# A two-layer Hyena, attention and experts kernel: Hyena filters computed in the head and at the joint, one column pass per group of modulation sections, the convolution's layer norm inside attention

## The chip, the cores and the metric

The kernel runs on one core of one Trainium2 chip. The metric is the device time of one execution in microseconds; the time before the change is 1821.3 us, the median of three runs (1820.79 to 1822.10). All arithmetic is in 32-bit floats.

## What is computed

Two layers work on 384 tokens of width 1024: 128 context tokens and 256 latent tokens, that is three tiles of 128 (NT = 3). Cut to what matters here, a layer is:

```python
mod = cond @ w_mod + b_mod                       # 6 sections of 1024, for two conditions
sh1, sc1, g1, sh2, sc2, g2 = split(mod, 6)
h = rms_norm(x) * (1 + sc1) + sh1
y = mixer(h)                                     # three groups side by side, then w_out
x = x + g1 * rms_norm(y)
h = rms_norm(x) * (1 + sc2) + sh2
x = x + g2 * rms_norm(moe(h))                    # 64 experts, 8 per token, and a shared one

# mixer: u = h @ w_in, cut into the columns of three groups
# convolution: a = u1 * sigmoid(u2); depthwise conv, 31 taps; layer_norm; silu
# Hyena: short conv; z = gate * (irfft(rfft(z) * kf) + bias * z), twice
# attention: four heads, difference of two softmaxes, rms_norm
# kf, from weights alone:
hid  = sin(fr * (feats @ hy_w1 + hy_b1))
hid  = sin(fr * (hid @ hy_w2 + hy_b2))
filt = (hid @ hy_w3) * window                    # forward and backward
kf   = rfft([fwd, 0, reversed bwd])
```

The Hyena filter and its spectrum depend on a layer's weights and on nothing else.

## The kernel before

Five engines run written-out programs, joined by semaphores; each program is in order. The work of a layer falls into stages.

**Modulation.** w_mod comes in 24 chunks of 2 MB (12 a layer), two for each section. `mod_chunk` (L616) multiplies a chunk by the padded condition (COND, 32 columns) into banks 6 and 7 of PSUM, four row groups of 32; after a section's second chunk ScalarE copies the rows out (`mod_rows`, L1271), TensorE folds them into columns with eight matmuls against FOLD (`mod_columns`, L606, "a column pass") and ScalarE copies the columns (`mod_column`, L1280). Chunks 0 to 3 (shift and scale of layer 0) are done in the head, chunks 4 to 15 in the attention of layer 0 (`fill`, L341: one chunk per unit) and 16 to 23 in that of layer 1. Their buffers are slot 0 of RING and KSYS in turn; SyncE reloads one once the chunk two before is used (`mod_in`, L381).

**Hyena filter.** `hidden` (L632, L1286, L1698) is one sine layer: a matmul, four VectorE operations and a Sin. `filters` (L641, L1708) makes the filter of one tile: two matmuls, then four VectorE operations with the windows, and the next tile's matmuls wait for them, since both use banks 1 and 2. `spectra` (L652, L1291) is the transform by matmuls, copied to KSYS by ScalarE. In layer 0 `hidden` runs in the head, in layer 1 behind the first two column tiles; in both layers `filters` stands behind tiles 2 to 4 and `spectra` behind tiles 5 to 7.

**Column tiles.** `u_tile` (L813) makes w_in's 19 outputs: ten in feature order with 128x384 results, nine in token order with 128x512. Between them stand the Hyena transforms (`z_turn`, `z_spectra`, `z_conv`), the mean and the variance of the convolution's layer norm (`conv_mean`, L713) and the turning of queries and keys (`qk_turn`). VectorE does the short convolution, the 31 taps, the rotary embedding and the gates.

**Layer norm of the convolution** (L1870 to L1888 on VectorE, L1371 to L1375 on ScalarE). It stands in front of attention in both programs: variance plus EPS, Sqrt on ScalarE, reciprocal, multiply, gain and bias, Sigmoid on ScalarE, multiply.

**Attention.** Twelve units (three tiles, four heads) in a pipeline of 14 iterations (L1093, L1377, L1890). An iteration of TensorE: scores of unit i, transpose of the weights of unit i - 1, column pass if there is one, a modulation chunk, pieces of w_out, values of unit i - 1, transpose of the output of unit i - 2. The scores of unit i wait for the exponentials of unit i - 1. GpSimd takes the power -0.5 of one column per unit (`power`, L509).

**Joint.** After the experts of layer 0, the sums of squares, the three residuals, the three normalisations and the transposes into feature order (`y_mean`, `residual`, `normalise`, `features`) lead to the first column tile of layer 1. GpSimd clears CB and RW there (`pads`, L575), behind its powers.

**Experts.** 34 steps a layer with 64 experts of 3 MB, the weights loaded during the steps. GpSimd makes a 128x384 comparison per step (`scat`, L522).

## Time and profile before

| What | us |
|---|---|
| median of three runs | 1821.3 |
| span of the profiled execution | 1822.1 |
| that execution's own time | 1823.92 |
| TensorE (PE) busy | 1705.8 (94%) |
| VectorE (DVE) busy | 617.4 (34%) |
| ScalarE (ACT) busy | 377.0 (21%) |
| GpSimd (POOL) busy | 187.2 (10%) |

Read it by stage: one share for the whole span is an average over stages in which different things are waited for. In the timelines a row is a start, a duration, an engine, the line and operation, what it writes and reads, how often, and in brackets how long the engine had been idle and what released it. A 32-bit matmul shows as two records.

### The profile page before, as it was taken

To read this page: it belongs to the slowest core of one execution; us is meant where nothing else is said; L and a number is where in the kernel's file an instruction comes from. 1 tells how busy PE (TensorE), PEld (TensorE's weight loads), DVE (VectorE), ACT (ScalarE), POOL (GpSimd) and SP (SyncE) were. 2 spreads that over 40 slices of the span, in tenths; PEclk is the share of its full clock that TensorE was granted. 3 is DMA by queue.
4 is the path that set the end of the run, shared out by engine and by line. 5 is a ranking of instruction groups with operands and counts; after the bars stand their busy time and mean duration, and the time that the engine had idled before them with its cause. 6 is when DMAs were issued, how large, how long until landed. Compare 5 with 4: busy or idle time off the path is not lost.

```text
span 1822.1 us, 22136 instructions
## 1 busy us (share of the span) xinstructions
PE 1705.8 (94%) x8440; PEld 824.3 (45%) x8440; DVE 617.4 (34%) x1669; ACT 377.0 (21%) x850; POOL 187.2 (10%) x193
## 2 busy tenths in 40 slices
PE   4999799989999999999959997999999999999995
PEld 2555345544444444444435553555444444444442
DVE  1358342422222222222154673433222222222223
ACT  2210343211111111111131014431111111111111
POOL 1000000011111111111110000100111111111110
PEclk9999889999999999999979998998999999999998
DMA  9212581198999999999832137315799999999993
GB/s 398 93 74 93 206 337 69 58 374 338 425 409 418 426 405 422 426 426 426 352 127 93 54 131 263 118 47 213 320 415 425 404 425 412 417 425 426 426 425 135
DMA packets 77147, 541.00 MB, mean 297 GB/s; under 512 B 8304, under 2 KB 11376, under 8 KB 21488
## 3 DMA queue, kind: packets, MB, share of 16 engines
q1 hardware_dynamic: 67248, 503.90, 67.4%
q0 software_dynamic: 9792, 35.66, 4.8%
q8 instruction: 69, 1.13, 0.2%
q14 instruction: 38, 0.31, 0.0%
HBM read 533.76 MB, written 5.77 MB: 296 GB/s over the span
## 4 chain that ended last, share of the span: by engine, by line
PE 87%; DMA 6%; DVE 3%; ACT 2%; issue 1%; SPq 0%; ACTq 0%; POOL 0%; DVEq 0%
PE PSB L836 29%; PE PSB L845 14%; PE PSB L828 7%; PE PSB L823 6%; PE PSB L890 5%; PE PSB L891 5%; PE PSB L791 4%; PE PSB L878 4%; PE PSB L626 2%; DMA RING<-in_wmod 2%; PE PSB L863 1%; DMA X<-in_x 1%; DMA WB<-in_exp_w_up 1%; DMA RING<-in_exp_w_up 1%; DMA KSYS<-in_wmod 1%; PE PSB L852 1%
## 5 line engine op out<-in xcount | busy, mean ns | idle before, releaser
L836 PE MATMUL PSB<-WB,EX 128*32 128x512 f32 (+2 forms) x1408 | 432.1, 598 | 0.2 <-DMA RING<-in_exp_w_up 0.2
L836 PE MATMUL PSB<-RING,EX 128*32 128x512 f32 (+2 forms) x1344 | 417.3, 598 | 3.8 <-DMA WB<-in_exp_w_up 2.1
L845 PE MATMUL PSB<-RING,AT 128*32 128x512 f32 (+2 forms) x720 | 229.8, 602 | 4.9 <-issue 3.8
L1647 DVE TENSOR_TENSOR YL<-PSB,YH 128x512 fp32r<-128x512 f32 x136 | 94.1, 692 | 354.5 <-ACT YH L1246 354.5
L845 PE MATMUL PSB<-WB,AT 128*32 128x512 f32 (+2 forms) x704 | 210.8, 596 | 0.0
L890 PE MATMUL PSB<-YH,SCAT 128*128 128x512 f32 x408 | 172.1, 422 | 2.8 <-DVE YL L1647 2.8
L836 PEld LDWEIGHTS PSB<-WB,EX 128*32 128x32 f32 (+2 forms) x1408 | 113.1, 126 | 136.0 <-issue 136.0
L526 POOL TENSOR_SCALAR SCAT<-CST,LSTT 128x384 fp32r<-128x384 f32 x68 | 85.2, 1252 | 841.6 <-PE PSB L891 841.5
L836 PEld LDWEIGHTS PSB<-RING,EX 128*32 128x32 f32 (+2 forms) x1344 | 105.8, 124 | 124.8 <-issue 124.8
L891 PE MATMUL PSB<-YL,SCAT 128*128 128x512 f32 x408 | 161.2, 395 | 0.0
L1629 DVE COPY EX<-PSB 128x512 f32<-128x512 f32 x68 | 47.0, 692 | 323.4 <-PE PSB L878 323.4
L1246 ACT ACTIVATE YH<-PSB 128x512 fp32r<-128x512 f32 x136 | 81.2, 597 | 239.6 <-PE PSB L845 239.6
L828 PE MATMUL PSB<-RING,HT 128*128 128x512 f32 x288 | 125.6, 592 | 0.0
L823 PE MATMUL PSB<-HT,RING 128*128 128x384 f32 x320 | 109.0, 495 | 3.3 <-ACT HT L1191 3.3
L878 PEld LDWEIGHTS PSB<-CST,XG 128*128 128x128 f32 x544 | 58.8, 141 | 106.9 <-issue 106.9
L845 PEld LDWEIGHTS PSB<-RING,AT 128*32 128x32 f32 (+2 forms) x720 | 63.5, 130 | 79.2 <-issue 79.2
L512 POOL TENSOR_TENSOR ST<-ST,HALF 128x1 f32<-128x1 f32 x48 | 26.4, 550 | 654.1 <-DVE ST L1911 476.6
L845 PEld LDWEIGHTS PSB<-WB,AT 128*32 128x32 f32 (+2 forms) x704 | 58.4, 126 | 72.4 <-issue 71.9
L1239 ACT ACTIVATE SGM<-PSB 128x256 f32<-128x256 f32 x68 | 26.1, 384 | 312.5 <-PE PSB L836 312.5
L878 PE MATMUL PSB<-CST,XG 128*128 128x128 f32 x544 | 88.2, 285 | 0.0
L890 PEld LDWEIGHTS PSB<-YH,SCAT 128*128 128x128 f32 x408 | 77.7, 190 | 21.6 <-issue 4.9
L791 PE MATMUL PSB<-RING,YT 128*128 128x512 f32 x192 | 85.0, 593 | 0.0
(262 smaller groups left out, 1779.0 us busy)
## 6 DMA issues: line engine op xcount, KB each, us to landing
RING<-in_exp_w_gate SPq DMA_DIRECT2D x64, 1024.0 KB, 10.5
RING<-in_exp_w_up SPq DMA_DIRECT2D x64, 1024.0 KB, 13.6
RING<-in_exp_w_down SPq DMA_DIRECT2D x64, 1024.0 KB, 14.1
WB<-in_exp_w_gate SPq DMA_DIRECT2D x64, 1024.0 KB, 11.8
WB<-in_exp_w_up SPq DMA_DIRECT2D x64, 1024.0 KB, 14.4
WB<-in_exp_w_down SPq DMA_DIRECT2D x64, 1024.0 KB, 14.1
RING<-in_wmod SPq DMA_DIRECT2D x14, 2048.0 KB, 10.0
KSYS<-in_wmod SPq DMA_DIRECT2D x10, 2048.0 KB, 9.3
```

What stands on the lines that cost most here:

```text
L526: nc.gpsimd.tensor_scalar(SCAT[:, s % 2, :], cst("iota"), LSTT[:, s:s + 1], None, ALU.is_equal).then_inc(p_scat, 1)
L791: mm = nc.tensor.matmul(PS[YB[0][t] + hf][:, :], YT[:, f, t * P:(t + 1) * P], w[:, f, :], start=(f == 0), stop=(f == 7))
L823: mm = nc.tensor.matmul(PS[3 + i % 3][:, 0:TOK], w[:, k, :], HT[:, k, :], start=(k == 0), stop=(k == KD - 1))
L828: mm = nc.tensor.matmul(PS[3 + i % 3][:, :], HT[:, k, t * P:(t + 1) * P], w[:, k, :], start=(k == 0), stop=(k == KD - 1))
L836: mm = nc.tensor.matmul(PS[6][s0:s0 + w, :].rearrange("p (w f) -> p w f", w=2), e[:, k, s0:s0 + w], rawgu[n % NBUF][:, k], start=(k == 0), ...
L845: mm = nc.tensor.matmul(dst[s0:s0 + w, :], AT[:, j, s0:s0 + w], rawdn[n % NBUF][:, hf, j], start=(j == 0), stop=(j == 1))
L878: mm = nc.tensor.transpose(PS[7][:, c * P:(c + 1) * P], XG[:, s % 2, k * P:(k + 1) * P], ident)
L890: nc.tensor.matmul(PS[piece][:, :], w, YHb[s % 2][:, cols], start=False, stop=False, skip_group_check=True)
L891: mm = nc.tensor.matmul(PS[piece][:, :], w, YLb[s % 2][:, cols], start=False, stop=True, skip_group_check=True)
L1246: sc.activation(YHb[s % 2][:, hf * 512:(hf + 1) * 512], PS[6 + hf][:, :], ACT.Copy).then_inc(a_yh, 1)
L1629: v.tensor_copy(EX2[:, s % 2, 4:8, :].rearrange("p k s -> p (k s)"), PS[7][:, :]).then_inc(e_high, 1)
L1647: v.tensor_tensor(YLb[s % 2][:, hf * 512:(hf + 1) * 512], PS[6 + hf][:, :], YHb[s % 2][:, hf * 512:(hf + 1) * 512].bitcast(F32), ALU.subtr ...
```

## The change

It has four parts.

1. The Hyena hidden layers, filters and spectra leave the column-tile stage. In layer 0 they stand between the four modulation chunks of the head, and the parameters are loaded ahead of the first chunk; in layer 1 the hidden layers, filters and the first spectrum stand between the steps of the joint, in banks 6 and 7, and the two other spectra behind the first two column tiles.
2. The modulation sections are taken in four groups (0 to 1, 2 to 5, 6 to 7, 8 to 11). The chunks of a group add into the same banks, each section's condition shifted to other rows, and a group has one copy of the rows and one column pass, with FOLD of up to eight columns.
3. The layer norm's end moves into the attention: GpSimd takes the power -0.5 of the variance (128x384) in one operation in place of Sqrt and reciprocal; VectorE normalises in iteration 4 (and applies gain and bias); ScalarE takes the exponential of the negative in iteration 5; VectorE makes 1/(1 + e) times the value in iterations 6 and 7, one half of the channels in each.
4. GpSimd clears only the padding columns, and for layer 1 right behind the experts, ahead of its powers of the joint.

```diff
-        COND = sb("COND", [P, KD, MT])
-        FOLD = sb("FOLD", [P, 2])
+        COND = sb("COND", [P, KD, MT + 6])
+        FOLD = sb("FOLD", [P, 8])
-        FTB = ((6, 0, 2), (4, 4, 4))
+        FTB = (((2, 6, 0), (4, 4, 4)), ((0, 2, 4), (4, 4, 4)))
+        HB = (0, 6)
+        SECS = ((0, 2), (2, 6), (6, 8), (8, 12))
 # SyncE
+                    sp.dma_start(PR[:, :], I["par"][0]).then_inc(par_in, 16)
                     mod_in(0)
-                    sp.dma_start(PR[:, :], I["par"][0]).then_inc(par_in, 16)
                     mod_in(1)
 # GpSimd
-                own.sig(nc.gpsimd.memset(CB[:, :, :], 0.0), p_pad)
-                own.sig(nc.gpsimd.memset(RW[:, :, :], 0.0), p_pad)
+                for first in (0, CPAD + P, 2 * CPAD + TOK):
+                    own.sig(nc.gpsimd.memset(CB[:, :, first:first + CPAD], 0.0), p_pad)
+                for first in (0, 1 + P, 2 + TOK):
+                    own.sig(nc.gpsimd.memset(RW[:, :, first:first + 1], 0.0), p_pad)
...
             for l in range(DEPTH):
+                pool.wait_ge(d_ln, K_LN * l + 5)
+                own.sig(nc.gpsimd.tensor_tensor(SG[:, 0, :], SG[:, 1, :], HALF[:, 0:1].to_broadcast([P, TOK]), ALU.pow), p_pow)
                 for u in range(NUN):
                     power(d_oms, NUN * l + u + 1, 24 + 2 * (u % 2), 1)
...
                 mixture_pool(l)
+                if l + 1 < DEPTH:
+                    pads()
 # TensorE
-            def mod_columns(sec):
+            def mod_columns(g):
+                first, last = SECS[g]
+                n = 2 * (last - first)
...
                 for k in range(KD):
-                    mm = nc.tensor.matmul(PS[5][:, 2 * k:2 * k + 2], MROWS[sec > 1][:, sec % 2, k * P:(k + 1) * P], FOLD[:, :],
+                    mm = nc.tensor.matmul(PS[5][:, n * k:n * (k + 1)], MROWS[g][:, k * P:(k + 1) * P], FOLD[:, 0:n],
...
+                at = 6 - 2 * (sec - first)
+                elif sec == first and part == 0:
+                    pe.wait_ge(a_mod, 2 * g)
-                        mm = nc.tensor.matmul(PS[6 + hf][MT * c:MT * (c + 1), :], COND[:, 4 * part + c, :],
-                                              w[:, c, hf * 512:(hf + 1) * 512], start=(part == 0), stop=(part == 1))
+                        mm = nc.tensor.matmul(PS[6 + hf][MT * c:MT * (c + 1), :], COND[:, 4 * part + c, at:at + MT],
+                                              w[:, c, hf * 512:(hf + 1) * 512], start=(sec == first and part == 0),
+                                              stop=(sec == last - 1 and part == 1), skip_group_check=True)
...
                 if l == 0:
                     pe.wait_ge(const_in, 16)
+                    hidden(l, 0)
+                    hidden(l, 1)
                     mod_chunk(0)
+                    filters(l, 0)
+                    filters(l, 1)
                     mod_chunk(1)
-                    hidden(l, 0)
-                    mod_columns(0)
+                    filters(l, 2)
+                    spectra(l, 0)
                     mod_chunk(2)
-                    hidden(l, 1)
+                    spectra(l, 1)
+                    spectra(l, 2)
                     mod_chunk(3)
-                    mod_columns(1)
-                    pe.wait_ge(d_arg, 8)
-                for t in range(NT):
-                    to_features(l, 0, t)
+                    mod_columns(0)
+                    to_features(l, 0, 0)
+                    to_features(l, 0, 1)
+                    pe.wait_ge(a_spec, 6 * (l + 1))
+                    to_features(l, 0, 2)
+                else:
+                    hidden(l, 0)
+                    hidden(l, 1)
+                    for t in range(NT):
+                        filters(l, t)
+                        to_features(l, 0, t)
+                    spectra(l, 0)
                 features_done(l, 0, 2)
                 for i in range(19):
                     u_tile(l, i)
                     if l > 0 and i < 2:
-                        hidden(l, i)
-                    if 2 <= i < 5:
-                        filters(l, i - 2)
-                    if 5 <= i < 8:
-                        spectra(l, i - 5)
+                        spectra(l, i + 1)
 # ScalarE, layer 1: hidden() behind the squares of y tiles 1 and 2; before attention gone:
-                act.wait_ge(d_ln, K_LN * l + 5)
-                own.sig(sc.activation(SG[:, 0, :], SG[:, 1, :], ACT.Sqrt), a_ln)
-                act.wait_ge(d_ln, K_LN * l + 10)
-                for c in range(2):
-                    own.sig(sc.activation(SG[:, c, :], CN[:, c, :], ACT.Sigmoid), a_ln)
...
+                    if i == 5:
+                        act.wait_ge(d_ln, K_LN * l + 9)
+                        for c in range(2):
+                            own.sig(sc.activation(SG[:, c, :], CN[:, c, :], ACT.Exp, scale=-1.0), a_ln)
-                    if j is not None and j % 2 == 1:
-                        mod_rows(j // 2)
+                    if j is not None and j + 1 in (12, 16, 24):
+                        mod_rows(GROUP[j // 2])
 # VectorE, layer 1, the joint
+                    scalars()
+                    hidden(l, 0)
+                    y_mean(l - 1, 1, 0)
                     modulation(l, 0, 2, MODR)
                     scale(0)
-                    y_mean(l - 1, 1, 0)
                     y_mean(l - 1, 1, 1)
                     residual(l - 1, 1, 0)
                     y_mean(l - 1, 1, 2)
+                    hidden(l, 1)
                     residual(l - 1, 1, 1)
                     normalise(l, 0, 0)
+                    filters(l, 0)
                     residual(l - 1, 1, 2)
                     normalise(l, 0, 1)
                     features(l, 0, 0)
+                    filters(l, 1)
                     normalise(l, 0, 2)
                     features(l, 0, 1)
+                    filters(l, 2)
                     features(l, 0, 2)
-                    scalars()
 # VectorE, layer norm
-                dve.wait_ge(a_ln, 3 * l + 1)
-                do(v.reciprocal(SG[:, 1, :], SG[:, 0, :]), d_ln)
...
+                def late_norm(n):
+                    if n == 0:
+                        dve.wait_ge(p_pow, POW[l, "cn"][0])
+                        for c in range(2):
+                            sig(v.tensor_tensor(CN[:, c, :], CN[:, c, :], SG[:, 0, :], ALU.mult), d_ln)
+                        own.wait(d_ln)
+                        for c in range(2):
+                            sig(v.tensor_scalar(CN[:, c, :], CN[:, c, :], par("lng")[:, c:c + 1], par("lnb")[:, c:c + 1],
+                                                ALU.mult, ALU.add), d_ln)
+                        return
+                    c = n - 1
+                    dve.wait_ge(a_ln, 2 * (l + 1))
+                    do(v.tensor_scalar(SG[:, c, :], SG[:, c, :], 1.0, None, ALU.add), d_ln)
+                    do(v.reciprocal(SG[:, c, :], SG[:, c, :]), d_ln)
+                    sig(v.tensor_tensor(YT[:, c, :], CN[:, c, :], SG[:, c, :], ALU.mult), d_ln)
...
+                    if i in (4, 6, 7):
+                        late_norm((4, 6, 7).index(i))
```

## Rows read from the trace of the kernel before

**Rows 1.** Busy time of each engine by stage; then granted clock, DMA share, GB/s.
```profile
0.00:50.00 50.00, 24.59 (x124) 12.38 (x124) 12.64 (x37) 14.58 (x30) 4.73 (x10) 0.97 0.95 388
50.00:204.50 154.50, 153.01 (x468) 84.02 (x469) 83.25 (x178) 20.56 (x49) 0.00 (x0) 1.00 0.23 85
204.50:290.00 85.50, 72.01 (x446) 35.75 (x447) 36.42 (x116) 37.22 (x119) 6.58 (x12) 0.84 0.78 295
...
390.00:919.00 529.00, 523.77 (x2904) 231.16 (x2903) 132.76 (x359) 86.46 (x170) 74.24 (x65) 1.00 0.96 401
919.00:945.00 26.00, 6.54 (x29) 5.24 (x28) 18.81 (x38) 13.11 (x31) 6.06 (x8) 0.61 0.56 222
```

**Rows 2.** TensorE's timeline in the head: chunk 1, chunk 3, first column tiles.
```profile
22.27 3.64 PE L626 MATMUL PSB<-RING,COND 128*32 128x512 f32 x16 [3.73 <-DMA RING<-in_wmod]
...
38.23 1.92 PE L626 MATMUL PSB<-RING,COND 128*32 128x512 f32 x16
...
50.09 15.72 PE L823 MATMUL PSB<-HT,RING 128*128 128x384 f32 x48 [1.81 <-ACT HT L1191]
```

**Rows 3.** Chain of waits, layer 0: hidden layer, one filter step, one spectrum.
```profile
37.52 0.80 PE PSB L639 x2
...
65.80 1.92 PE PSB L648 x4
...
94.50 3.43 PE PSB L665 x8
```

**Rows 4.** VectorE's timeline: parameters' first use, a hidden layer, one filter.
```profile
17.43 0.14 DVE L1811 TENSOR_SCALAR ST<-PR 64x1 f32<-64x1 f32 x1 [7.10 <-DMA PR<-in_par]
...
27.49 0.67 DVE L1703 TENSOR_SCALAR CO<-PSB,ST 64x384 f32<-64x384 f32 x1 [8.82 <-PE PSB L636]
...
29.17 0.35 DVE L1706 TENSOR_SCALAR CO<-CO 64x384 f32<-64x384 f32 x1
...
67.83 0.69 DVE L1714 TENSOR_TENSOR QKV<-PSB,CST 128x512 f32<-128x512 f32 x1 [16.67 <-PE PSB L648]
...
69.76 0.68 DVE L1717 TENSOR_TENSOR QKV<-QKV 128x512 f32<-128x512 f32 x1
```

**Rows 5.** SyncE's issues of modulation chunks in layer 0's attention.
```profile
218.85 0.35 SPq L388 DMA_DIRECT2D KSYS<-in_wmod  x1
225.13 0.33 SPq L388 DMA_DIRECT2D RING<-in_wmod  x1
```

**Rows 6.** Timeline of the joint, VectorE, GpSimd, TensorE.
```profile
935.26 0.75 DVE L1449 TENSOR_SCALAR YT<-X,ST 128x1024 f32<-128x1024 f32 x1 [0.73 <-POOL ST L512]
...
938.08 3.17 DVE L1449 TENSOR_SCALAR YT<-X,ST 128x1024 f32<-128x1024 f32 x1 [0.73 <-POOL ST L512]
938.67 2.04 POOL L578 MEMSET RW<- 128x2322 f32 x1
...
944.79 7.22 PE L823 MATMUL PSB<-HT,RING 128*128 128x384 f32 x16 [1.51 <-ACT HT L1191]
```

**Rows 7.** Timeline of layer 0's attention, VectorE and TensorE.
```profile
206.35 2.55 DVE L1879 RECIPROCAL SG<-SG 128x384 f32<-128x384 f32 x1 [12.76 <-ACT SG L1372]
...
214.46 0.80 PE L1100 MATMUL PSB<-KT,QT 64*128 64x128 f32 x4 [7.60 <-ACT HT L1389]
...
219.72 1.85 PE L612 MATMUL PSB<-FOLD,CO 128*128 128x2 f32 x16
...
232.98 3.64 PE L626 MATMUL PSB<-RING,COND 128*32 128x512 f32 x16 [1.34 <-DMA RING<-in_wmod]
...
278.08 1.92 PE L626 MATMUL PSB<-KSYS,COND 128*32 128x512 f32 x16 [1.09 <-DMA KSYS<-in_wmod]
```

**Rows 8.** GpSimd's groups of the whole span: count, busy us, mean ns, idle before.
```profile
L526 POOL TENSOR_SCALAR SCAT<-CST,LSTT 128x384 fp32r<-128x384 f32 x68 | 85.2, 1252 | 841.6 <-PE PSB L891 841.5
...
L512 POOL TENSOR_TENSOR ST<-ST,HALF 128x1 f32<-128x1 f32 x48 | 26.4, 550 | 654.1 <-DVE ST L1911 476.6 <-DVE ST L1462 110.3 <-DVE ST L1447 67.2
```

More of the change, by code:

```diff
@@ L339, in build @@
         SLOT_OF = {key: (a, i + 1) for a, use in enumerate(SLOT_USE) for i, key in enumerate(use)}
+        SECS = ((0, 2), (2, 6), (6, 8), (8, 12))
+        GROUP = {s_: g_ for g_, (a_, b_) in enumerate(SECS) for s_ in range(a_, b_)}
         def fill(l, i):
             first, n = (4, 12) if l == 0 else (16, 8)
-            return first + i if i < n else None, (first + i) // 2 - 1 if 0 < i <= n and i % 2 == 0 else None
+            ended = {8: 1, 12: 2} if l == 0 else {8: 3}
+            return first + i if i < n else None, ended.get(i)
         def pieces(l, i):
@@ L618, in mod_chunk @@
                 a, n = SLOT_OF["m", j]
-                part = j % 2
+                sec, part = divmod(j, 2)
+                g = GROUP[sec]
+                first, last = SECS[g]
+                at = 6 - 2 * (sec - first)
                 if j == 0:
                     pe.wait_ge(d_cond, 3)
+                elif sec == first and part == 0:
+                    pe.wait_ge(a_mod, 2 * g)
                 pe.wait_ge(chunk_in[a], 16 * n)
@@ L647, in filters @@
                 for half in range(2):
-                    mm = nc.tensor.matmul(PS[1 + half][:, :], HID[:, 4, t * P:(t + 1) * P],
+                    mm = nc.tensor.matmul(PS[HB[l] + half][:, :], HID[:, 4, t * P:(t + 1) * P],
                                           par("w3", 64)[:, half * 512:(half + 1) * 512], start=True, stop=True)
@@ L660, in spectra @@
                         w = cst("cf1" if part == 0 else "sf1")
-                        mm = nc.tensor.matmul(PS[1 + part][:, :], w, f[:, 0, :], start=True, stop=True)
+                        mm = nc.tensor.matmul(PS[HB[l] + part][:, :], w, f[:, 0, :], start=True, stop=True)
                     else:
@@ L664, in spectra @@
                         for t in range(2):
-                            mm = nc.tensor.matmul(PS[1 + part][:, :], w[:, t, (q - 1) * P:q * P], f[:, 1 + t, :],
+                            mm = nc.tensor.matmul(PS[HB[l] + part][:, :], w[:, t, (q - 1) * P:q * P], f[:, 1 + t, :],
                                                   start=(t == 0), stop=(t == 1))
@@ L1294, in spectra @@
                 for part in range(2):
-                    own.sig(sc.activation(KS[:, q, part, :, :].rearrange("p o n -> p (o n)"), PS[1 + part][:, :], ACT.Copy), a_spec)
+                    own.sig(sc.activation(KS[:, q, part, :, :].rearrange("p o n -> p (o n)"), PS[HB[l] + part][:, :], ACT.Copy), a_spec)
             def z_out(l, o):
@@ L1332, in _ @@
                 if l == 0:
+                    hidden(l, 0)
+                    hidden(l, 1)
                     for t in range(NT):
                         squares(l, 0, t)
+                    for q in range(NT):
+                        spectra(l, q)
                     mod_rows(0)
-                    hidden(l, 0)
                     mod_column(0)
-                    hidden(l, 1)
-                    mod_rows(1)
-                    mod_column(1)
                     act.wait_ge(d_mod, 3)
@@ L1347, in _ @@
                             y_squares(l - 1, 1, t, hf)
+                        if t > 0:
+                            hidden(l, t - 1)
                     squares(l, 0, 0)
@@ L1354, in _ @@
                     features(l, 0, 2)
+                    spectra(l, 0)
                 act.wait_ge(d_fr, 5 * (l + 1))
                 own.sig(sc.activation(ST[:, 34:36], ST[:, 32:34], ACT.Exp), a_lam)
[L1358 removed]
+                act.wait_ge(p_pad, 6 * (l + 1))
                 for i in range(19):
@@ L1361, in _ @@
                     if l > 0 and i < 2:
-                        hidden(l, i)
-                    if 5 <= i < 8:
-                        spectra(l, i - 5)
+                        spectra(l, i + 1)
                     if i in (8, 13):
@@ L1820, in _ @@
                     hidden(l, 0)
+                    hidden(l, 1)
+                    for t in range(NT):
+                        filters(l, t)
                     for t in range(NT):
                         normalise(l, 0, t)
-                    hidden(l, 1)
                     modulation(l, 0, 2, MODC)
@@ L1834, in _ @@
                     y_mean(l - 1, 1, 2)
+                    hidden(l, 1)
                     residual(l - 1, 1, 1)
                     normalise(l, 0, 0)
+                    filters(l, 0)
                     residual(l - 1, 1, 2)
```

90 lines of the change are left out of this document (39 added, 51 removed).

## The prediction

> **What bounds the kernel now.** I read the busy table by stage first [rows 1]. The reader is to see two kinds of stage. The expert stages (390 to 919 us, and its twin in layer 1) hold TensorE 99% busy at the full clock; the change touches nothing in them, so they move as a block, and what is won or lost ahead of each goes into the end one to one. So do the column-tile stages (50 to 204.5 us; layer 1 repeats it): TensorE 153.0 of 154.5 us. In between lie three places where TensorE idles: the head (24.6 busy of 50), the joint of the layers (6.5 of 26) and attention (72.0 of 85.5, at a mean granted clock of 0.84). The change moves work from the full stages into the idle ones.
>
> The other views then give prices: TensorE's timeline in the head [rows 2], the chain of waits through the tile stage [rows 3], VectorE's steps for the Hyena filter [rows 4], the SyncE queue [rows 5], the joint [rows 6], attention [rows 7] and GpSimd's groups [rows 8]. The sum is made against the profiled execution (span 1822.1, its own time 1823.9), and goes on to the median 1821.3 as a difference. A measurement of this kernel can tell about 0.2%, 3.6 us, from no change.
>
> **Layer 0: tile stage shorter, head longer.** Out of the tile stage go three filter steps at 1.92, two spectra at 3.43 and a first spectrum with half of their matmuls, 1.72 [rows 3]: 5.76 + 1.72 + 6.86 = 14.3 us of a path that had no gap. VectorE's steps go with them; nothing in the tiles waited for them.
>
> They come back in the head, where they form a chain with VectorE. The parameters now land before the first chunk; they are 1 MB behind a chunk in a queue in which they arrived at 17.4 [rows 4], so with the chunk (5 us) taken out, at about 12.5. Hidden layer 1: TensorE to 14, VectorE's four operations 2.03 us (27.49 to 29.52 [rows 4]), Sin 0.5: 16.7. Hidden layer 2 the same: its matmul to 18.3, Sin done at 20.9. Chunk 0 meanwhile, then filter 0. From here each filter waits for VectorE's four operations on the one before, 2.61 us (67.83 to 70.44 [rows 4]), with a chunk in one of the two gaps. Chunks cost 3.64 at the low clock and 1.92 at the high one [rows 2], and the other matmuls scale likewise. With the filters and the first chunks at about 2.4 each, between the levels: filter 0 ends at 24.3, filter 1 at 29.5, chunk 1 at 31.9, filter 2 at 34.5, spectrum 0 (after VectorE) at 39.8. Then TensorE has no more gaps and I take the high clock: chunk 2 at 42.0, spectra 1 and 2 at 48.8, chunk 3 at 50.8. Chunk 3's load now starts only once chunk 1 is used (31.9) and takes 7.9 us, as the load issued at 225.13 and awaited until 232.98 does [rows 5, 7]: hidden. Row copies and one column pass instead of two (1.85 [rows 7]): 53.3. Modulation, the 12 evictions (4.5 us) and the start of the tiles: 59.6 against 50.09 now [rows 2]. The head costs 9.5, the stage gives 14.3: **-4.8**. Ends: all of the filter part and no more at the low clock gives 65.5 (+15.4, net +1.1); all at the high clock 57.5 (net -7).
>
> **Joint.** Out of layer 1's tile stage go three filters, spectrum 0 and two hidden matmuls at 0.80: 5.76 + 1.72 + 1.6 = 9.1 [rows 3]. VectorE is the chain of the joint: it is 18.8 of 26 us busy [rows 1], and takes on the hidden steps (2 x 2.03), three filters (3 x 2.7 with their waits) and the scalars (1.25), 13.4 us. It gets back 2.4: the whole-tile memset on GpSimd (2.04 us) lies beside the normalise that took 3.17 where its sisters take 0.75 [rows 6]; the new pads are a few columns, done earlier. Walking the new order with these prices (first residual done at 928.0, second at 933.2, filter 0 at 937.7, third residual at 940.7, filter 1 at 946.5, filter 2 at 952.6, last features at 954.0, and spectrum 0 on TensorE to 955.3) the first tile starts some 10.5 us later than 944.79. Part of the 7.22 us of that tile is low clock [rows 6] and may go; I count nothing for most of it: **+1.0**, between -3 and +5. ScalarE's extra load of the Sin table (1.3) lies beside VectorE's residuals.
>
> **Attention, twice.** Today the layer norm stands in front of the first unit: Sqrt, a 2.55 us reciprocal at 206.35, Sigmoid and the tables between them, and TensorE waits 7.60 us, to 214.46, for the first exponentials [rows 7]. It had ended chunk 0 at 206.86, so the first scores were there 1.92 before, at 204.94. Without the norm in front their maximum is taken at once, the exponentials are there at about 206.5 and hidden behind chunk 0, and chunk 1, already loaded, ends at 209.8 instead of 218.85, when its slot is reloaded [rows 5]. That is 9.0 us. Then the loads decide: 10 chunks of 2.1 MB at 401 GB/s [rows 1] are 5.2 us each, while TensorE's busy 72.0 us over twelve units, less six column passes, is 5.1 a unit with the slow stretches in it [rows 1, 7], so some 4.0 to 4.7 at the high clock. Walking it (a load starts when the chunk two before is used, 7.9 us for one alone, 5.2 behind another, the chunk at 3.64 after each wait) I find chunk 2 used at 218.7 (before 225.1 [rows 5]), chunk 6 at 242, chunk 8 at 253, and the last at 271 against 280.0 now (278.08 + 1.92 [rows 7]). So of 9.0 won and four column passes dropped (4 x 1.85 = 7.4 [rows 7]) about 9 arrives; the column passes mostly shorten waits that loads set anyway. Late norm on VectorE: 1.9 us in iteration 4, then 0.6 + 2.55 + 0.5 in iterations 6 and 7 beside 3.0 of its own (36.4 over twelve [rows 1]), against 4.5 to 5 on TensorE: up to 2 us show (those small operations are estimates from neighbours of the same size; the reciprocal is the row's). **-8.5** in layer 0; in layer 1, eight chunks and three passes dropped, **-7.5**. Bounds 4 to 13 each.
>
> The power on GpSimd, 128x384, is in no row. Below: the same shape compared, 1.25 us; above: 384 times the one-column power of 0.55, 211 us [rows 8]. In that one column most will be fixed cost, so I take the row of the same shape times some ten, 12 us. Its operand is ready at 193.6 (VectorE's 12.76 us of idle time before 206.35 begin there [rows 7]); behind it in GpSimd's queue stand the powers of attention, the first due at about 211 and, since chunk 2 holds TensorE until 218.7, free to come by 218. Up to 24 us cost nothing; VectorE's normalise, due in iteration 4 (225), neither.
>
> The Trainium skill (GPSIMD Engine Reference, section 3.1) has a two-operand add of 2048 columns at 4497 ns; by that, as an estimate, 384 columns are 0.8 us and the sum stays. No run here shows that for a power.
>
> **Sum:** -4.8 + 1.0 - 8.5 - 7.5 = -19.8: 1801.5.
>
> **Rivals.** (a) *The broken head keeps the low clock.* In the head chunks ran at 3.64 after a 3.73 us gap although the granted clock reads near 1 [rows 1, 2]; the new chain has three gaps of 2.6 us. Then the head is +15.4 and the joint's matmuls add 2: 6 + 2 more, 1809.5. Against it: once no gap is left, chunks run at 1.92 again [rows 2]. The Trainium skill (TensorE: Matmul & The Clock Gate, Part 1) holds that the throttled state is the default and only sustained activity releases it; that speaks for this rival. Chance 0.18. (b) *Loads take back attention's gain*: every chunk waits, runs at 3.64, and the next load starts late, as at 232.98 [rows 7]. Only 4 a layer remain: 1809.5 as well. Chance 0.17. (c) *Loads at full rate*: 13 and 10 in attention: 1794.5. Chance 0.12. (d) **Slower: GpSimd's power.** Place: the wait for the first attention power in each layer. Beyond 24 us all of it is on the path, twice; from 34 us the change loses. At 50 us: 2 x 26 - 19.8 = +32, 1853. For it: the upper bound of 211; against it: no row prices a column. Chance 0.08. (e) *The work merely changes place*: head +1.1, joint +5, attention 4 a layer: -1.9, 1819.5. Chance 0.04. My forecast keeps 0.41.
>
> **Numbers.** The range 1789 to 1814 takes in the forecast, (a), (b), (c) and the bounds of both heads, and leaves out (d) and (e). Faster by over 0.2% means under 1817.7: 0.88; same 0.04; slower 0.08.
>
> **What would show it.** Right: first tile at 58 to 62; layer 0's tiles end 14 us sooner after their start; no wait of 7.6 before the second scores in either layer; four column passes instead of 12; waits of TensorE on chunk loads larger than now; last features of the joint near 954. Wrong: a power on GpSimd over 24 us with VectorE's L1928 waiting for it; a first tile beyond 66; chunks of attention consumed no earlier than now from the fourth on; or the expert stages changing length at all.

## The result, and the profile after

The changed kernel takes 1891.76 us (median of four runs, 1888.82 to 1897.49) beside 1821.05 us of the kernel before: ratio 1.0391, 95% interval 1.0367 to 1.0414. It is 71 us slower, where 1801.5, 20 us faster, was forecast. The profiled execution has a span of 1887.0 us and a time of its own of 1888.82.

GpSimd's groups of the changed kernel (count, busy us, mean ns of one, idle time before) show the new operation; [rows 8] had no such line.

```profile
L598 POOL TENSOR_TENSOR SG<-SG,HALF 128x384 f32<-128x384 f32 x2 | 123.1, 61534 | 297.2 <-DVE SG L1908 297.2
L517 POOL TENSOR_TENSOR ST<-ST,HALF 128x1 f32<-128x1 f32 x48 | 26.4, 550 | 279.4 <-DVE ST L1947 101.8 <-DVE ST L1491 90.7 <-DVE ST L1476 86.9
```

The power on 128x384 takes 61.5 us. GpSimd's timeline in layer 0 (start, duration):

```profile
194.39 61.53 POOL L598 TENSOR_TENSOR SG<-SG,HALF 128x384 f32<-128x384 f32 x1 [151.23 <-DVE SG L1908]
255.91 0.54 POOL L517 TENSOR_TENSOR ST<-ST,HALF 128x1 f32<-128x1 f32 x1
258.49 0.55 POOL L517 TENSOR_TENSOR ST<-ST,HALF 128x1 f32<-128x1 f32 x1 [2.04 <-DVE ST L1947]
```

The first power of attention stands behind it and runs at 255.91, where the kernel before had it at 219.99. Who waits is in the table of waits (us in total, times, longest):

```profile
DVE RW L1964 <- POOL ST L517: 91.9, 6, 44.4
...
PE PSB L1157 <- DVE RW L1964: 69.6, 2, 35.3
```

VectorE's L1964 scales unit 0's output by that power and waits 44.4 us. TensorE then waits for VectorE, because the values of unit 1 (L1157) go into the bank that L1964 still has to read. TensorE's timeline in attention, layer 0 and then layer 1:

```profile
205.66 1.92 PE L643 MATMUL PSB<-RING,COND 128*32 128x512 f32 x16
...
208.53 1.92 PE L643 MATMUL PSB<-KSYS,COND 128*32 128x512 f32 x16
...
218.26 3.50 PE L643 MATMUL PSB<-RING,COND 128*32 128x512 f32 x16 [6.71 <-DMA RING<-in_wmod]
257.05 0.76 PE L1157 MATMUL PSB<-QKV,HT 128*128 128x128 f32 x2 [35.29 <-DVE RW L1964]
...
1186.35 0.77 PE L1157 MATMUL PSB<-QKV,HT 128*128 128x128 f32 x2 [34.28 <-DVE RW L1964]
```

The two waits of 35.3 and 34.3 us are 69.6 us, nearly as much as the kernel lost; the table below shows where the rest of the change cancels out. The stages of the changed kernel, as [rows 1] (head, tiles, attention, part of the experts, joint):

```profile
0.00:64.03 64.03, 38.31 (x140) 15.15 (x141) 20.43 (x49) 16.89 (x33) 2.29 (x14) 0.89 0.76 303
64.03:205.24 141.21, 139.79 (x437) 79.29 (x437) 75.50 (x166) 17.29 (x43) 10.85 (x1) 0.99 0.25 93
205.24:311.12 105.88, 54.02 (x360) 23.51 (x361) 38.18 (x109) 28.69 (x100) 56.70 (x12) 0.77 0.61 238
411.00:943.00 532.00, 523.73 (x2896) 230.92 (x2897) 131.83 (x361) 87.86 (x170) 74.25 (x65) 1.00 0.98 405
950.00:987.00 37.00, 23.40 (x47) 10.38 (x47) 28.82 (x61) 14.19 (x33) 3.68 (x12) 0.57 0.39 156
```

To compare kernels I cut every profile at the same seven points: first column tile, first scores, first piece of w_out and last matmul of the experts in layer 0, and the first three again in layer 1. Lengths in us, each from one profiled execution ("experts" holds the rest of w_out, routing and experts; the last column goes up to the end):

| kernel | head | tiles | att. 0 | experts 0 | joint | tiles 1 | att. 1 | last |
|---|---|---|---|---|---|---|---|---|
| before | 50.1 | 154.4 | 78.3 | 636.3 | 25.7 | 158.2 | 54.8 | 664.2 |
| after | 64.0 | 141.2 | 105.9 | 638.9 | 37.0 | 147.5 | 87.3 | 665.1 |
| w96 | 69.1 | 141.2 | 71.5 | 638.6 | 36.6 | 146.3 | 53.5 | 662.0 |
| col | 59.5 | 141.2 | 76.5 | 636.4 | 36.9 | 146.3 | 53.4 | 665.0 |
| col_four | 67.3 | 141.2 | 64.5 | 641.9 | 36.7 | 146.3 | 51.6 | 664.3 |
| before_four | 50.5 | 155.9 | 71.9 | 641.7 | 25.6 | 159.1 | 53.4 | 660.5 |
| col_tiles01 | 46.6 | 154.4 | 74.7 | 638.3 | 23.2 | 159.0 | 54.4 | 664.2 |
| col_tiles01_four | 47.2 | 154.4 | 63.8 | 638.9 | 23.2 | 159.3 | 51.6 | 664.5 |

Of the 64.9 us by which the span grew, the attentions have 60.0; head and tiles of layer 0 together +0.7, joint and tiles of layer 1 +0.6, the two expert stages 2.6 and 0.9.

### The profile page after: what moved, and what is told of

The parts are those of the page before. It is cut to its first block, busy times and chain, and to the rows that moved or that the text cites. A ratio compares the mean times of both kernels' runs of the same rounds, so it can differ in the third digit from the quotient of the medians.

```text
span 1887.0 us, 21858 instructions
## 1 busy us (share of the span) xinstructions
PE 1697.1 (90%) x8312; PEld 810.7 (43%) x8312; DVE 621.3 (33%) x1675; ACT 361.4 (19%) x820; POOL 305.6 (16%) x203
## 3 DMA queue, kind: packets, MB, share of 16 engines
q1 hardware_dynamic: 67248, 503.90, 65.5%
## 4 chain that ended last, share of the span: by engine, by line
PE 76%; DMA 10%; POOL 7%; DVE 4%; issue 1%; ACT 1%; SPq 0%; DVEq 0%; ACTq 0%
PE PSB L854 26%; PE PSB L863 12%; POOL SG L598 7%; PE PSB L846 6%; PE PSB L841 6%; DMA RING<-in_exp_w_up 5%; PE PSB L908 4%; PE PSB L809 4%; PE PSB L909 4%; PE PSB L896 4%; DMA WB<-in_exp_w_up 4%; PE PSB L643 2%; PE PSB L881 1%; DMA KSYS<-in_wmod 1%; PE PSB L870 1%
## 5 line engine op out<-in xcount | busy, mean ns | idle before, releaser
L598 POOL TENSOR_TENSOR SG<-SG,HALF 128x384 f32<-128x384 f32 x2 | 123.1, 61534 | 297.2 <-DVE SG L1908 297.2
L863 PEld LDWEIGHTS PSB<-RING,AT 128*32 128x32 f32 (+2 forms) x720 | 63.8, 130 | 80.2 <-issue 80.1
L524 POOL DMA_INDIRECT XG<-h_rows,IDX x68 | 70.0, 1030 | 121.9 <-DVE LSTW L1628 95.6
L1266 ACT ACTIVATE SGM<-PSB 128x256 f32<-128x256 f32 x68 | 26.1, 384 | 312.7 <-PE PSB L854 312.7
```

The lines of the kernel that those rows point to most:

```text
L598: own.sig(nc.gpsimd.tensor_tensor(SG[:, 0, :], SG[:, 1, :], HALF[:, 0:1].to_broadcast([P, TOK]), ALU.pow), p_pow)
L863: mm = nc.tensor.matmul(dst[s0:s0 + w, :], AT[:, j, s0:s0 + w], rawdn[n % NBUF][:, hf, j], start=(j == 0), stop=(j == 1))
```

## The experiments

Every ratio is to the kernel before, on the same chip (it is worked out from all runs and can differ a little from the quotient of two medians). The first four ask what the power costs and what is left of the change without it.

**w96 and w192: the power on fewer columns.** The scale of the other columns is left out.

```diff
-tensor_tensor(SG[:, 0, :], SG[:, 1, :], HALF[:, 0:1].to_broadcast([P, TOK]), ALU.pow)
+tensor_tensor(SG[:, 0, 0:96], SG[:, 1, 0:96], HALF[:, 0:1].to_broadcast([P, 96]), ALU.pow)
```

> The changed kernel with GpSimd's power taken on 96 of its 384 columns (the scale of the other columns is left out). Theory Q (the power's length, queued ahead of attention's powers, is what costs): the power took 61.5 us for 384 columns, 160 ns a column, so here about 15.4 us if it is a price per column; that is under the 24 us that the walk in the prediction called free. The two TensorE waits of 35.3 and 34.3 us for the first short-conv rows of attention are gone (under 3 us each), and attention turns from +27.5 and +32.5 us against the kernel before into about -7 each: 1808, between 1800 and 1822. Rival H (head, joint or the late norm itself lose most of it): stays above 1840. Rival S (most of the 61.5 is a fixed cost of a power of many columns, like loading a routine): the power stays above 40 us and the time above 1850.

> The same on 192 of 384 columns. Theory Q: the power takes 30.8 us; the free span of 24 us is passed by some 7 us, so each layer loses about 5 to 7 us against the 96-column kernel: 1818 to 1824, with TensorE waits for the conv rows of about 5 us. Rival H: the time moves by less than 3 us between 96 and 192 columns and lies above 1840. Rival S: power above 45 us.

(The rows called short-conv rows in these texts are attention's outputs; they lie in the short convolution's buffer.) Measured: w96 1820.88 us, 1.0003 (0.9992 to 1.0014); w192 1831.75 us, 1.0059 (1.0034 to 1.0084). GpSimd's timelines, w96 first, then w192 with its next power:

```profile
199.47 15.64 POOL L598 TENSOR_TENSOR SG<-SG,HALF 128x96 f32<-128x96 f32 x1 [152.17 <-DVE SG L1908]
```

```profile
189.91 30.93 POOL L598 TENSOR_TENSOR SG<-SG,HALF 128x192 f32<-128x192 f32 x1 [148.55 <-DVE SG L1908]
220.83 0.54 POOL L517 TENSOR_TENSOR ST<-ST,HALF 128x1 f32<-128x1 f32 x1
```

15.64, 30.93 and 61.53 us for 96, 192 and 384 columns: 159 ns a column and 0.3 us besides, to within 0.1 us. Rivals S and H (a fixed cost, and a loss elsewhere) are out. From the times the free span comes out twice: w192 lost 1831.75 - 1820.88 = 10.9 us against w96, 5.4 a layer, so 30.9 - 5.4 = 25.5 us were free; the full width lost 70.9 (medians of two chips), 35.4 a layer, so 26.1 were free. The prediction's 24 was nearly right. TensorE's waits in w192 (5.01 us in layer 0, 9.7 over both) say the same. But w96 is at 1821, 13 us above the 1808 expected and at the upper end of its range: without the power's cost the change gains nothing. That is a second failure of the forecast, hidden under the first.

**col: the whole computation with a cheap power.** The variance is taken with tokens on partitions, the power is 128x3, and three matmuls spread it over the features.

```diff
+for t in range(NT):
+    for c in range(2):
+        matmul(PS[2][:, t:t + 1], SG[:, c, t * P:(t + 1) * P], cst("mean")[:, 0:1], ...)
-tensor_tensor(SG[:, 0, :], SG[:, 1, :], HALF..., ALU.pow)
+tensor_tensor(ST[:, 9:12], ST[:, 60:63], HALF..., ALU.pow)
+for t in range(NT):                                   # TensorE, iteration 1
+    matmul(PS[5][:, (t + 1) * P:(t + 2) * P], ST[:, 9 + t:10 + t].to_broadcast([P, P]), ident, ...)
```

> The whole computation, with the power on three columns: the variance goes through TensorE with tokens on partitions (six small matmuls), GpSimd raises 128x3 to the power -0.5 (about 0.55 to 1 us by the one-column powers) and three matmuls spread the result over the features into PSUM, where the late norm reads it; no reciprocal on VectorE. Theory Q: as the 96-column kernel, some 1806, between 1798 and 1815, so about 85 us under the changed kernel and 10 to 20 under the kernel before. Rival H: above 1840. Rival L (the chunk loads take attention's gain): 1812 to 1822, with larger TensorE waits for DMA in attention.

Measured: 1820.06 us, 0.9992 (0.9978 to 1.0006), the power at 0.857 us. 72 us are back. Theory Q's range ended at 1815; the time lies in the one that the text gives to rival L. TensorE's timeline in layer 0's attention shows what took the place of the 7.60 us of [rows 7]:

```profile
204.69 1.92 PE L643 MATMUL PSB<-KSYS,COND 128*32 128x512 f32 x16
213.79 3.23 PE L643 MATMUL PSB<-RING,COND 128*32 128x512 f32 x16 [6.08 <-DMA RING<-in_wmod]
...
238.52 3.64 PE L643 MATMUL PSB<-RING,COND 128*32 128x512 f32 x16 [4.65 <-DMA RING<-in_wmod]
...
270.77 3.38 PE L643 MATMUL PSB<-KSYS,COND 128*32 128x512 f32 x16 [2.81 <-DMA KSYS<-in_wmod]
```

and SyncE's issues say why the third chunk was late:

```profile
197.94 0.33 SPq L405 DMA_DIRECT2D RING<-in_wo  x1
...
203.13 0.35 SPq L393 DMA_DIRECT2D RING<-in_wmod  x1
```

Chunk 2 (the first chunk of attention is chunk 0) is issued at 203.13 and can be used at 213.8, 10.7 us later; 2 MB of w_out, issued 5 us earlier, are still on the way. With the queue empty or nearly so such a load took 7.5 to 7.9 us in these traces. The 4.65 us wait at 238.52 is another matter: that load, issued at 226.78, took 11.7 us, although the one before it had landed by 229.7, and the same load took 7.7 and 7.6 us in the two profiles of col_tiles01 and col_tiles01_b below. Part of this profile's waiting is peculiar to this execution. Over layer 0's attention TensorE waits 18.1 us for chunks (5.6 before), over layer 1's 11.3 (4.9 before).

**early: the layer norm back in front of attention**, nothing wide on GpSimd.

```diff
-own.sig(nc.gpsimd.tensor_tensor(SG[:, 0, :], SG[:, 1, :], HALF..., ALU.pow), p_pow)
-if i in (4, 6, 7): late_norm(...)
+own.sig(sc.activation(SG[:, 0, :], SG[:, 1, :], ACT.Sqrt), a_ln)       # ahead of unit 0
+reciprocal, gain and bias, Sigmoid and product as in the kernel before
```

> The changed kernel with the layer norm of the conv back in front of attention as before (Sqrt on ScalarE, reciprocal and Sigmoid ahead of the first unit, no wide power on GpSimd). Theory Q: no 35 us waits; the 7.6 us wait before the second scores is back in both layers, so it lies 5 to 18 us above the column-power kernel and keeps head, joint and grouped column passes: 1812 to 1824, near the kernel before. Rival N (the late norm gives nothing because the loads set attention's pace): within 4 us of the column-power kernel. Rival H: above 1840.

Measured: 1823.6 us, 1.0019 (0.9998 to 1.0039), at the upper end of theory Q's range but only 3.5 us above col, which is rival N's case; the 7.60 us wait is back. The pair is taken up again below.

**Hyena steps back among the tiles, and slots for the loads.** col_tiles01 is col with both layers' filters and spectra where the kernel before has them. col_four is col with four slots for chunks in place of two, before_four the kernel before with the same edit, and col_four_cols is col_four with six idle column passes:

```diff
-hidden, filters, spectra in the head and at the joint          # col_tiles01
+hidden, filters (tiles 2 to 4), spectra (tiles 5 to 7), as in the kernel before
-slots 0 and 3: alternate chunks; 2 and 1: w_out after the tiles    # the four slots
+[("m", j) for j in (4, 8, 12, 14)] ...                     # slot 0
+... ("m", 7), ("m", 11), (0, "o1") ...                     # slot 1
+... ("m", 6), ("m", 10), (0, "o0") ...                     # slot 2
+[("m", j) for j in (5, 9, 13, 15, 17, 21, 23)]             # slot 3
+order of issue: 8, 9, 10, 11, 12, 13, o0, o1, 14, 15; layer 1: 20, 21, o0, o1, 22, 23
+for k in range(16):                                            # col_four_cols, six times
+    matmul(PS[5][:, 64 + 2 * (k % 8):66 + 2 * (k % 8)], ident, ident[:, 0:2], ...)
```

> The column-power kernel with the weight slots of attention given out differently: four slots in rotation for the modulation chunks in place of two; chunks 2 and 3 of each attention are loaded during the end of the column tiles, and the two halves of w_out after chunks 6 and 7 of attention. Theory L (the loads took attention's gain; in the column-power kernel TensorE waited 18.1 us in layer 0's attention and 11.3 us in layer 1's for chunks, against 5.6 and 4.9 in the kernel before): these waits fall to under 4 us in each, attention goes from 76.5 and 53.4 us to about 66 and 46, and the time to about 1804, between 1798 and 1811. Rival V (VectorE's chain with the late norm, or TensorE's clock, would set attention's length anyway): waits for DMA fall but waits for VectorE or matmuls at the low clock take their place, and the time stays above 1813.

> The kernel before with the same four slots and nothing else. Theory L: it has little wait on loads to lose (5.6 and 4.9 us in the two attentions) and keeps the 7.6 us wait for the first exponentials and its column passes: 1812 to 1819, so that the changed parts are worth 8 to 13 us once the loads are out of the way. Rival V: it gains as much as the column-power kernel gains from the slots, to within 3 us.

> The column-power kernel with the Hyena filters and spectra put back among the column tiles in both layers (grouped columns, late norm and pads stay). Theory: the move is worth about nothing. Stage by stage: head back to 50 us and tiles to 154, first scores at about 204.5, where the kernels with the move had 200.7 to 210.3 according to TensorE's clock in the head; joint plus tiles of layer 1 within 1 us. So within 4 us of the column-power kernel, 1816 to 1826, and less scatter between its runs. Rival P (the move is worth the 10 us forecast: head -4.8, joint +1 and less low clock): over 5 us slower than the column-power kernel. Rival M (the move costs): under 1814.

> The kernel with four slots and the column power, plus six idle column passes of 16 two-column matmuls in attention (four in layer 0, two in layer 1), as the ungrouped sections had. In the kernel before such a pass took 1.85 us. If TensorE is now what sets attention's pace, they cost 6 x 1.85 = 11 us against the four-slot kernel; if loads or VectorE's chain set it, under 4 us.

Measured: col_four 1815.08 us, 0.9962 (0.9945 to 0.9978); before_four 1813.73, 0.9965 (0.9952 to 0.9978); col_tiles01 1815.35, 0.9970 (0.9957 to 0.9983); col_four_cols 1818.49, 0.9989 (0.9976 to 1.0002).

The slots shorten layer 0's attention from 76.5 to 64.5 us, about as theory L had it. The waits for chunks do not fall under 4 us, however: they are 6.7 us in layer 0 (18.1 before) and 11.0 in layer 1, as good as unchanged, and layer 1's attention goes from 53.4 to 51.6 us where 46 was expected:

```profile
PE PSB L651 <- DMA RING<-in_wmod: 11.0, 1, 11.0
```

That one chunk is issued behind both halves of w_out and takes 18.2 us to land (TensorE's wait in layer 1's attention is the row above). In the time of the whole only 0.30% arrives, and before_four gains as much (0.35%). Rival V's mark is met. The granted clock shows where some of it went. The first 22.8 us after attention in col:

```profile
277.19:300.00 22.81, 22.81 (x85) 12.69 (x85) 5.48 (x26) 7.61 (x15) 1.10 (x2) 1.00 0.00 1
```

and in col_four:

```profile
272.98:295.80 22.82, 22.82 (x77) 12.42 (x78) 3.84 (x23) 5.75 (x13) 1.10 (x2) 0.87 0.00 1
```

TensorE has no gap in either, and is granted 0.87 in the second. From the end of attention to the end of layer 0's experts, col takes 636.4 us and col_four 641.9. That the shorter attention is the cause is not shown: the best kernel below is as short in attention and takes 638.9. The idle column passes cost 1818.49 - 1815.08 = 3.4 us. Each has 16 matmuls where a pass of the kernel before has 8, and takes 3.63 us and not the 1.85 of its expectation:

```profile
229.93 3.63 PE L1168 MATMUL PSB<-CST 128*128 128x2 f32 x32
```

So six of them keep TensorE busy for 22 us, twice what was meant, and are still mostly hidden, even with four slots.

The Hyena move costs: col is at 0.9992, col_tiles01 at 0.9970 (another chip, each against its own kernel before), and so it is in two further pairs: early at 1.0019 and early_tiles01 (below) at 0.9997, col_four at 0.9962 and col_tiles01_four (below) at 0.9915. That is 0.2% with two slots and 0.5% with four, so theory "worth about nothing" was too kind to it. In the profiles, head and tiles of layer 0 took 200.7 to 210.3 us in the seven profiled kernels with the move and no idle matmuls (mean 206.1) and 201.0 to 206.0 in the six with grouped columns and without the move (mean 202.4). The spread with the move is TensorE's clock: over these seven profiles the same matmuls of the head are busy for 33.1 to 43.3 us, the first tile starts at 59.5 to 69.1, and the two rise together. The head of w96 (first tile at 69.11):

```profile
23.03 3.78 PE L666 MATMUL PSB<-PR,CO 64*128 64x512 f32 x4
29.59 3.78 PE L666 MATMUL PSB<-PR,CO 64*128 64x512 f32 x4 [2.78 <-DVE QKV L1746]
33.30 3.64 PE L643 MATMUL PSB<-RING,COND 128*32 128x512 f32 x16
```

and of col, the same program up to there (first tile at 59.54):

```profile
22.47 1.98 PE L666 MATMUL PSB<-PR,CO 64*128 64x512 f32 x4
27.24 2.33 PE L666 MATMUL PSB<-PR,CO 64*128 64x512 f32 x4 [2.78 <-DVE QKV L1761]
29.50 3.22 PE L643 MATMUL PSB<-RING,COND 128*32 128x512 f32 x16
```

**col_warm, the best kernel, and grouping alone.** col_warm puts 15 idle matmuls into the head's gaps; col_tiles01_four joins the two gains; early_tiles01 is the kernel before with grouped columns and narrow pads only.

```diff
+for _ in range(4):
+    nc.tensor.matmul(PS[3][:, :], ident, CST[:, 0:512], start=True, stop=True)
 filters(l, 1)
```

> The column-power kernel with 15 idle matmuls (128x512, into a bank that is free then) put on TensorE in the head, in front of the first hidden step, between the hidden steps, between filter 0 and 1 and ahead of spectrum 0, where it waits 2.8 to 4.1 us for VectorE or ScalarE. Theory C (the head's length hangs on TensorE's granted clock: first tile at 59.5 us in the run whose matmuls of the head went over to the high clock at the second filter, 69.1 in the run in which they stayed at 3.78 us each): with the gaps filled the filters take 1.99 us each from filter 1 on, the first tile starts between 58 and 61 us although matmuls were added, and the median is 2 to 6 us under the column-power kernel. Rival G (the idle matmuls only lengthen the chain at the low clock): first tile later than 66, median equal or up to 5 us above it.

> Column power, grouped columns, late norm and pads kept; Hyena steps back among the tiles; four slots for the chunks. If the two gains found so far add (Hyena steps back: 0.2% better than the column-power kernel; four slots: 0.3%), 1809 to 1813, under both kernels. Rival V (what waits lose, the low clock after attention takes back): 1814 to 1817, no better than the slots or the tiles alone.

> The kernel before with only the grouped modulation columns and the narrower pads: layer norm ahead of attention, Hyena steps among the tiles, two slots. The grouping drops one column pass in the head (1.85 us, with its row copies: first tile at 46.6 us in the column-power kernel with tiles, against 50.1 in the kernel before) and four and two passes of 1.85 us in the attentions, which loads cover. Expected 2 to 5 us under the kernel before: 1815 to 1818. If the late norm is what brought the 5 us of the column-power kernel with tiles, this one lies within 2 us of the kernel before.

Measured: col_warm 1814.69 us, 0.9973 (0.9963 to 0.9984); **col_tiles01_four 1805.7 us, 0.9915 (0.9895 to 0.9935)**; early_tiles01 1820.25, 0.9997 (0.9987 to 1.0006). In col_warm every filter runs at the high clock from the first on:

```profile
23.98 1.99 PE L666 MATMUL PSB<-PR,CO 64*128 64x512 f32 x4 [0.88 <-ACT CO L1343]
25.89 3.70 PE L1085 MATMUL PSB<-CST 128*128 128x512 f32 x8
29.52 1.99 PE L666 MATMUL PSB<-PR,CO 64*128 64x512 f32 x4
```

The first tile comes at 62.58, above the 58 to 61 expected: four idle matmuls last 3.70 us where the gap was 2.78, so they were too many. The median's ratio is 0.19% lower than col's, as theory C had it; but the two kernels ran on different chips and the intervals overlap, so this gain is likely and not shown.

col_tiles01_four beats both kernels, 15 us under the one and 86 under the other, and lies below the 1809 to 1813 expected; with six runs it has the widest interval of these three. Grouping the columns and narrowing the pads is worth nothing that can be measured, where 2 to 5 us were expected, although the joint shortens as forecast (25.7 to 23.2 us) and both attentions together take 127.3 and 127.6 us in two profiles (133.2 before). The expert stages take part of it back, as the account of the prediction below shows.

**What the late norm is worth.** The medians gave it 0.27% on the pair early and col, but the profiled attentions of such pairs were equally long. So:

> The kernel before with grouped columns, narrower pads and the four slots, the layer norm still ahead of attention. Against the best kernel so far (the same with the late norm and the column power, 0.9915 of the kernel before) it prices the late norm where loads bind little. If the late norm is worth what the forecast said, the 7.6 us wait of both layers less 2 us of VectorE's steps, it lies 9 to 12 us above, near 1815 to 1817. If attention without the wait only turns into low clock and waits for VectorE, it lies within 4 us, 1806 to 1810.

> The kernel with only grouped columns and pads again, beside the next one on one chip. With two slots the late norm was worth 0.27% on two pairs of kernels, but the profiles do not show it in attention (127.6 us for both attentions with the norm in front, 129.1 with the late norm). If it is real it comes again: 4 to 6 us above the next kernel. If it was the difference of chips: within 2 us.

> The column-power kernel with the Hyena steps among the tiles again, as the pair of the kernel above; and a second look at where attention's length comes from. If loads set it with two slots: both attentions together 127 to 131 us again, with over 20 us of TensorE waits for chunks.

Measured: early_tiles01_four 1811.47 us, 0.9952 (0.9936 to 0.9969); early_tiles01_b 1819.09, 0.9995 (0.9977 to 1.0013); col_tiles01_b 1813.64, 0.9963 (0.9943 to 0.9982). On one chip the late norm is worth 5.5 us with two slots, so it was no difference of chips. With four slots it is 5.8 us by the medians and 6.7 by the ratios (the two kernels ran on different chips), between the two cases of the expectation, for two waits of 7.60 us removed. The second profiles have it in attention too: both attentions 127.3 us with the norm in front, 123.0 with it late, although 127 to 131 were expected again; the waits for chunks are over 20 us (25.5), as expected. The first profiles had said 127.6 and 129.1. Single profiles of the attentions of one kernel differ by 6 us.

## Why the prediction was wrong

**GpSimd's power: the step that failed.** The prediction bounded it by 1.25 and 211 us, held that "in that one column most will be fixed cost", and took ten times the comparison's row, 12 us. It measured 61.5. Of the 0.550 us of one column 0.159 are the column's own work and 0.39 fixed, so the fixed share was indeed most, 71%; but the other 29% times 384 is 61 us. The row to scale from was the same operation on one column, with an unknown fixed share: to be free, a column had to cost under 24 / 384 = 62 ns, a fixed share of 89%, and nothing in the trace said that. The add of the Trainium skill (GPSIMD Engine Reference, section 3.1: 4497 ns for 2048 columns) would give, as an estimate, 0.8 us for 384, a factor of 73 under the row for the power; what it says of an add does not carry to a power.

**What hangs on the power** was right: the place, who waits, the free span (24 forecast; 25.5 and 26.1 from the measured times) and the consequence. Rival (d) is the case that came; by its own sum it gives 2 x (61.5 - 24) - 19.8 = +55.2, 1876.5. The remaining 15 us are the second failure.

**Attention, twice: -8.5 and -7.5; the term that failed is the landing time of its first reload, and it is a part of the miss only.** In col's profile attention is -1.9 and -1.5. The wait for the exponentials did vanish, and chunk 1 was done 5.5 us after the first scores (4.9 forecast). Then the sum took 7.9 us for the next load, from a row where it travelled alone; here it shared the queue with w_out and took 10.7. The trace of the kernel before had that price: the same load, issued at 206.92 behind w_out, took 11.1 us there, unseen, because no one waited for it.

```profile
201.73 0.33 SPq L400 DMA_DIRECT2D RING<-in_wo  x1
...
206.92 0.35 SPq L388 DMA_DIRECT2D RING<-in_wmod  x1
```

Chunk 2 was done 15.9 us after the scores (13.8 forecast): 2.1 of the 7.0 us by which the last chunk was late (73.0, 66 forecast, 75.1 before). Chunk 6, with the slow load of this one execution, was 4.0 late. What made up the rest was not taken apart, and in a single profile it is within the 6 us scatter: both attentions together took 129.8 us in col, 125.0 in w96 and 123.0 in col_tiles01_b, against 133.2 before and 117.2 forecast. Rival (b), with 4 us left a layer, was the right mechanism and, within that scatter, of the right size. By medians the late norm brings 5.5 us over both layers with two slots.

**Column passes**: twelve became four, and the time stayed (0.9997). The prediction half said so ("mostly shorten waits that loads set anyway"), but that was not the whole reason, as the next paragraph shows.

**The expert stages: "they move as a block", at nothing; a premise that failed.** The prediction held that what is won ahead of them "goes into the end one to one", and named a changed length as a sign of being wrong. The sign is there. From the first scatter matmul of the experts to the last, in us, the kernel before took 504.1 and 504.7 and before_four 504.8 and 505.4; the other fourteen profiles, all with grouped columns and narrow pads, have 506.4 to 509.3, in every one of their 28 stages (before_four and three of the fourteen ran on one chip, so it is no difference of chips). Here the kernel before and then early_tiles01, which has nothing but those two parts:

```profile
414.79:918.87 504.08, 501.84 (x2834) 220.19 (x2834) 125.33 (x337) 83.22 (x163) 70.72 (x62) 1.00 0.97 402
```

```profile
411.42:919.19 507.77, 503.27 (x2834) 220.49 (x2834) 125.32 (x337) 83.21 (x163) 70.76 (x62) 1.00 0.97 400
```

The clock is 1.00 in both. TensorE's waits for the experts' weights, all of them late in a stage, from some 390 us on, are 0.8 us in the one and 3.1 in the other (0.8 to 2.1 over the four stages, 1.8 to 4.2 over the 28). That is some 2.4 us a layer, near 5 of the 20 us that went missing. Which of the edits slows those loads or starts them later was not tried.

**Head: +9.5 forecast, +13.9 measured in the changed kernel's profile**, +9.4 to +19.0 over the profiles with the move and no idle matmuls. The value forecast, 59.6, is the one with the early high clock (59.5 in col, 59.6 in w192); five of the seven profiles lie above it. Rival (a) has its upper end at 65.5; w96 passes it, since there the slow stretch reached from chunk 0 to spectrum 0. The tiles gave 13.2 of 14.3. The rule that went with rival (a) (the Trainium skill, TensorE: Matmul & The Clock Gate, Part 1: the throttled state is the default, sustained work releases it) agrees with this and with col_warm.

**Joint: +1.0.** Measured +0.6 with the tiles. The walk of VectorE's order was nearly exact; from the end of the experts, in us (forecast, then the changed kernel): first residual 8.9, 8.9; second 14.1, 14.1; filter 0 18.6, 18.3; filter 2 33.5, 33.3; last features 34.9, 34.7. The normalise that took 3.17 us beside the old memset takes 0.75 like its sisters [rows 6].

**The parts, by the medians** (ratios to the kernel before, two slots): grouping and pads 0.9997 and 0.9995; with the late norm and a cheap power 0.9970 and 0.9963; with the Hyena move 0.9992; with the wide power 1.0391. One part gains 0.3%, one loses 0.2%, one loses 4%. Of the 20 us forecast the sum had 16 in the late norm's and the passes' attention and 4 in the Hyena move and joint; 5.5 came of the first, and the second turned into a small loss.

## What to carry to other kernels

When an operation moves to an engine that has only run it on one column, split that row's time into a fixed and a per-column part before scaling; if no second size exists, price it from the full upper bound and ask how long the engine's queue may be blocked. Take a load's landing time from the place where it will be issued, also where nothing waits for it yet. Compare the length even of the stages that a change leaves alone. Put statistics of tokens on partitions, where a power is three columns wide, and spread the result with matmuls. When a wait goes away, look at which load is issued right behind it and what else is in the queue at that moment: here two more slots for the loads, none of them new memory, brought 0.3 to 0.55%.

## What the runs showed that was not expected

GpSimd's power costs 159 ns a column of 128 partitions, linear from 96 to 384 columns; the same engine's comparison on 384 columns takes 1.25 us in all [rows 8].

TensorE's matmuls in the head run at 3.78 or 1.98 us for the same filter in two executions of the same instructions, but the granted clock of the two heads reads almost alike. The head of w96 and then that of col (granted clock third from the end):

```profile
0.00:69.11 69.11, 43.29 (x141) 16.40 (x141) 20.36 (x49) 16.60 (x33) 2.28 (x14) 0.98 0.70 281
```

```profile
0.00:59.54 59.54, 33.18 (x141) 12.70 (x141) 20.35 (x49) 16.19 (x33) 2.28 (x14) 0.97 0.80 325
```

The same 141 matmuls are 43.29 us busy in one and 33.18 in the other: the durations tell it, the mean clock of the stretch does not.

After attention, with no gap in its work, TensorE was granted 0.87 in col_four and 1.00 in col. Why was not settled.
